# Five token tiles for six meet all experts, and the gathered rows serve three tiles and the samples

## What is computed

```python
s = jnp.einsum('thpd,hpnd->thpn', q, sub_keys)
top_s, top_i = lax.top_k(s, PEER_TOPK)
cand_s = top_s[:, :, 0, :, None] + top_s[:, :, 1, None, :]
cand_i = top_i[:, :, 0, :, None] * PEER_KEYS + top_i[:, :, 1, None, :]
...
fin_s, pos = lax.top_k(cand_s, PEER_TOPK)
fin_i = jnp.take_along_axis(cand_i, pos, axis=-1)
gate = jax.nn.softmax(fin_s, axis=-1)
...
act = jax.nn.gelu(jnp.einsum('tkd,td->tk', expert_u[ik], xk))
return jnp.einsum('tk,tkd->td', gk * act, expert_v[ik])
```

## Time and profile before

| | us |
|---|---|
| median of three runs | 3489.68 |
| the profiled execution | 3483.48 |
| its span | 3481.6 |
| TensorE busy | 3275.2 (94%) |
| TensorE weight loads | 2876.5 (83%) |
| VectorE busy | 2557.4 (73%) |
| ScalarE busy | 922.7 (27%) |
| GpSimd busy | 807.6 (23%) |
| moved | 695.59 MB |

### The profile page before, as it was taken

How to read it: one execution, slowest core, us unless ns; L and a number is a source line. 1 busy time by engine, 2 the same in 40 slices (tenths; PEclk the granted TensorE clock), 3 DMA queues, 4 the chain that set the end, 5 groups by cost and what they waited for, 6 DMA issues and landing times. The chain is left out here.

```text
span 3481.6 us, 46050 instructions
## 1 busy us (share of the span) xinstructions
PE 3275.2 (94%) x17777; PEld 2876.5 (83%) x17777; DVE 2557.4 (73%) x5373; ACT 922.7 (27%) x1336; POOL 807.6 (23%) x639
## 2 busy tenths in 40 slices
PE   6999989689999999989999999976999999999996
PEld 5867755389999999989999999975888888888885
DVE  4621253421299999988888888866899888989986
ACT  3210300311122222224444444432222222222222
POOL 1000000000001110113333333322344443444431
PEclk8999989799999999999999999998999999999998
DMA  5020021211134444448889889878888888888884
GB/s 93 16 38 27 13 96 53 91 56 39 41 128 144 144 143 142 144 137 274 305 286 332 305 299 329 285 279 317 302 303 293 298 304 303 295 299 300 305 298 135
DMA packets 329539, 695.59 MB, mean 200 GB/s; under 512 B 30869, under 2 KB 191449, under 8 KB 323161
## 3 DMA queue, kind: packets, MB, share of 16 engines
q1 hardware_dynamic: 244824, 386.01, 32.2%
q0 software_dynamic: 84496, 306.64, 26.4%
HBM read 580.12 MB, written 110.64 MB: 198 GB/s over the span
## 5 line engine op out<-in xcount | busy, mean ns | idle before, releaser
L1731 POOL DMA_INDIRECT dr_row<-in_peer_v_dram,idx x288 | 425.7, 1478 | 665.9 <-DVE acc_s L1750 655.0
L1731 POOL DMA_INDIRECT gr_row<-in_peer_u_dram,idx x240 | 290.4, 1210 | 464.2 <-DVE raw L1740 442.0
L1750 DVE SCALAR_TENSOR_TENSOR acc_s<-dr_row,gate,acc_s 128x1024 f32<-128x1024 f32 x288 | 367.2, 1275 | 0.0
L2263 DVE TENSOR_TENSOR acc<-pd_po,acc 128x512 f32<-128x512 f32 x384 | 264.0, 687 | 120.7 <-PE pd_po L2296 120.7
L1740 DVE CUSTOM_DVE_ANT_0 gr_row<-gr_row,xs 128x1024 f32<-128x1024 f32 x240 | 288.3, 1216 | 0.0
L2149 ACT ACTIVATE pg_wb<-pg_pw 128x512 f32<-128x512 f32 x192 | 210.8, 1099 | 56.6 <-PE pg_pw L2127 51.2
L486 PE MATMUL fr_a<-pj_w,h_t 128*128 128x256 f32 (+1 forms) x864 | 198.4, 392 | 17.3 <-PEq L184 17.3
L2106 DVE TENSOR_SCALAR pg_hot_i<-pg_iota,sel_t 128x128 f32<-128x128 f32 x768 | 212.8, 355 | 0.0
L486 PEld LDWEIGHTS fr_a<-pj_w,h_t 128*128 128x128 f32 (+1 forms) x864 | 170.3, 227 | 45.0 <-issue 23.1
L2127 PE MATMUL pg_pw<-pg_hot_i,pg_hot_j 128*128 128x128 f32 x1536 | 203.3, 276 | 3.0 <-DVE pg_hot_i L2106 3.0
L2127 PEld LDWEIGHTS pg_pw<-pg_hot_i,pg_hot_j 128*128 128x128 f32 x1536 | 194.8, 192 | 3.4 <-DVE pg_hot_i L2106 3.4
(11 more groups left out here) (487 smaller groups left out, 7972.0 us busy)
## 6 DMA issues: line engine op xcount, KB each, us to landing
pd_v<-in_peer_v_dram SPq DMA_DIRECT2D x128, 512.0 KB
w_d<-pg_wb SPq DMA_DIRECT2D x48, 1024.0 KB
pd_w<-w_d SPq DMA_DIRECT2D x64, 768.0 KB, 6.8
pd_a<-act_d SPq DMA_DIRECT2D x64, 768.0 KB, 9.2
ta_u<-in_peer_u_dram SPq DMA_DIRECT2D x64, 512.0 KB
ga_u<-in_peer_u_dram SPq DMA_DIRECT2D x64, 512.0 KB
act_d<-ta_a SPq DMA_DIRECT2D x128, 192.0 KB
act_d<-ga_a SPq DMA_DIRECT2D x128, 192.0 KB
```

What stands on the lines that cost most here:

```text
L1731: pool.indirect_dma_start(self.buf[i % self.n][:], None, self.table, bass.IndirectOffsetOnAxis(ap=self.idx[:, col:col + 1], axis=0)).then_ ...
L1750: self.nc.vector.scalar_tensor_tensor(out=out, in0=self.buf[i % self.n][:], scalar=w[:, col:col + 1], in1=out, op0=ALU.mult, op1=ALU.add). ...
L2263: nc.vector.tensor_tensor(out, po[(OUTS * g + o) % NPO][:], out, ALU.add).then_inc(o_added, 1)
```

## The change

ND goes from 6 to 5 and NSP from 2 to 3; the widths follow (TD 640, WB 320, COLS 416, BANKS 160, OUTS 10, ten chunks of w_d). The numbers 7 and 14 of the choice become UP_A_TILE = 8 and 16, so that 73 expert tiles run beside the choice and 55 in the gates. The gates loop counts steps of the expert tiles (165) and not groups; groups_at gives a step its groups such that all 160 are made in the first 147 steps; the last chunk is written at step 149. In the down stage SP loads four tiles ahead of acc, GpSimd waits for three products before its first fetch, and the twelve preparations of a group are spread over ten outputs. A buffer that holds the keys and then sel_t gets a shared room. TensorE's and ScalarE's loops in the gates are rewritten like VectorE's.

```diff
-ORDER = (2, 3, 4, 5, 6, 7, 0, 1, 8)
-ND = 6
+ORDER = (3, 4, 5, 6, 7, 0, 1, 2, 8)
+ND = 5
 TD = ND * P
-NSP = 2
+NSP = 3
...
-UP_TOPK = 7 * NT + 1
+UP_A_TILE = 8
+UP_TOPK = UP_A_TILE * NT + 1
 UP_GATES = NK - UP_TOPK
...
-CHOICE = (6, 7, 8, 0, 1, 2, 3, 4, 5)
+CHOICE = tuple(range(ND, NT)) + tuple(range(ND))
+NS = NT - ND
...
-    return min(2 * (UP_TOPK - 2), 14 * q + 14 * (point + 1) // POINTS)
+    return min(2 * (UP_TOPK - 2), 2 * UP_A_TILE * q + 2 * UP_A_TILE * (point + 1) // POINTS)
...
-                if q > 3:
-                    pe.wait_ge(stored, q - 3)
+                if q > NS:
+                    pe.wait_ge(stored, q - NS)
...
+STEPS = 3 * UP_GATES
+EARLY = 18
+
+
+def groups_at(s):
+
+    return range(min(BANKS, BANKS * s // (STEPS - EARLY)), min(BANKS, BANKS * (s + 1) // (STEPS - EARLY)))
...
-            for g in range(BANKS):
-                n, k = g // 3, g % 3
-                if n < UP_GATES:
-                    if k == 1:
-                        up.keep(sp, n, 0)
-                        if n + 2 < UP_GATES:
-                            up.load(sp, n + 2)
-                    if k == 2:
-                        up.keep(sp, n, 1)
-                c, b = g // BC - 1, g % BC
-                if c >= 0 and b < PIECES:
-                    if b == 0:
-                        sp.wait_ge(stored, (c + 1) * BC)
-                    write(c, b)
-            sp.wait_ge(stored, BANKS)
-            for piece in range(PIECES):
-                write(NCH - 1, piece)
+            for s in range(STEPS):
+                n, k = s // 3, s % 3
+                if k == 1:
+                    up.keep(sp, n, 0)
+                    if n + 2 < UP_GATES:
+                        up.load(sp, n + 2)
+                if k == 2:
+                    up.keep(sp, n, 1)
+                for g in groups_at(s):
+                    c, b = g // BC - 1, g % BC
+                    if c >= 0 and b < PIECES:
+                        if b == 0:
+                            sp.wait_ge(stored, (c + 1) * BC)
+                        write(c, b)
+                if s == STEPS - EARLY + 2:
+                    sp.wait_ge(stored, BANKS)
+                    for piece in range(PIECES):
+                        write(NCH - 1, piece)
...
+            for s in range(STEPS + 2):
+                if s < STEPS:
+                    for g in groups_at(s):
+                        one_hots(g)
...
+                    for i in range(NR * s // STEPS, NR * (s + 1) // STEPS):
                         rows_u.dot(dve, i, xs, raw)
...
-            load(0)
-            load(1)
+            for m in range(GE):
+                load(m)
             for s in range(ND):
...
-            for m in range(2, NK):
+            for m in range(GE, NK):
                 load(m)
...
             nc.gpsimd.memset(acc_s[:, NSP, :], 0.0).then_inc(accs_zero, 1)
+            pool.wait_ge(mul, GE - 1)
             for i in range(COLS):
                 rows_v.fetch(pool, i)
...
-                    m = GE * (g + 1) + o // 3
-                    if m < NK:
-                        (multiply, low_v, low_w)[o % 3](m)
+                    for p in range(3 * GE * o // OUTS, 3 * GE * (o + 1) // OUTS):
+                        m = GE * (g + 1) + p // 3
+                        if m < NK:
+                            (multiply, low_v, low_w)[p % 3](m)
                     add(g, o)
```

More of the change, by code:

```diff
@@ L1858, in _ @@
                     exponent(ex_after[n])
-                for q in range(3, NT):
+                for q in range(NS, NT):
                     if turned_after(q) == n:
@@ L1993, in _ @@
                 settle()
-                if q > 3:
-                    dve.wait_ge(turned, q - 3)
+                if q > NS:
+                    dve.wait_ge(turned, q - NS)
                 for i in range(2):
@@ L2095, in _, with one_hots @@
             dve.wait_ge(shaped, 1)
[L2096 to L2110, removed]
+            def one_hots(g):
+                if g >= NHB:
+                    dve.wait_ge(made, g - NHB + 1)
+                hb = g % NHB
+                nc.vector.tensor_tensor(hot_j[:, hb], iota[:].unsqueeze(1).broadcast_to([P, BT, P]),
+                                        sel_t[:, 1, g * BT:(g + 1) * BT].unsqueeze(2).broadcast_to([P, BT, P]),
+                                        ALU.is_equal)
+                for j in range(BT):
+                    tok = slice(g * BT + j, g * BT + j + 1)
+                    ins = nc.vector.tensor_scalar(hot_i[:, hb, j, :], iota[:], sel_t[:, 0, tok], sel_t[:, 2, tok],
+                                                  ALU.is_equal, ALU.mult)
+                ins.then_inc(hot, 1)
+            for s in range(STEPS + 2):
+                if s < STEPS:
+                    for g in groups_at(s):
+                        one_hots(g)
+                n, k = (s - 2) // 3, (s - 2) % 3
+                if s >= 2 and k == 1 and n + 1 < UP_GATES:
                     up.low(dve, n + 1, 0)
                     up.low(dve, n + 1, 1)
-                if g < BANKS:
-                    for i in range(NR * g // BANKS, NR * (g + 1) // BANKS):
+                if s < STEPS:
+                    for i in range(NR * s // STEPS, NR * (s + 1) // STEPS):
                         rows_u.dot(dve, i, xs, raw)
@@ L2121, in _ @@
                 up.turn(pe, 0, half)
[L2122 to L2126, removed]
-                    mm = nc.tensor.matmul(pw[g % 2][:, j, :], hot_j[:, g % NHB, j, :], hot_i[:, g % NHB, j, :],
-                                          start=True, stop=True)
-                mm.then_inc(made, 1)
-                n, k = g // 3, g % 3
-                if n < UP_GATES:
-                    if k == 0:
-                        up.up(pe, n, 0)
-                    if k == 1 and n + 1 < UP_GATES:
-                        up.turn(pe, n + 1, 0)
-                        up.turn(pe, n + 1, 1)
-                    if k == 2:
-                        up.up(pe, n, 1)
+            for s in range(STEPS):
+                for g in groups_at(s):
+                    pe.wait_ge(hot, g + 1)
+                    if g >= 2:
+                        pe.wait_ge(stored, g - 1)
+                    for j in range(BT):
+                        mm = nc.tensor.matmul(pw[g % 2][:, j, :], hot_j[:, g % NHB, j, :], hot_i[:, g % NHB, j, :],
+                                              start=True, stop=True)
+                    mm.then_inc(made, 1)
+                n, k = s // 3, s % 3
+                if k == 0:
+                    up.up(pe, n, 0)
+                if k == 1 and n + 1 < UP_GATES:
+                    up.turn(pe, n + 1, 0)
+                    up.turn(pe, n + 1, 1)
+                if k == 2:
+                    up.up(pe, n, 1)
         @block.scalar
```

45 lines of the change are left out of this document (23 added, 22 removed).

## The result

The changed kernel takes **3566.28 us** (median of 4 runs, 3559.26 to 3571.14), the one before 3491.23 beside it: ratio 1.021, 95% interval 1.0183 to 1.0237. It is 75 us slower; 3473 was predicted, the range ended at 3530, and "slower" had 0.24. The profiled execution took 3571.14 us, its span 3569.3.

What follows compares the result with a forecast made beforehand. The prediction took VectorE to bound the gates and down loops after the change. Its terms, norm and scores +1, choice +8, gates +18, boundary -8, down stage -36, finish 0, sum to -17: 3473 us, range 3425 to 3530.

Steps and rivals of the forecast that it cites:

- 582: Gates loop: TensorE's busy time after the change, forecast at 582 us for 763.
- Norm, choice, boundary, the start of the down stage: Norm and scores +1 us, choice +8, boundary -8; in the down stage TensorE starts near 20 us, VectorE adds from 33.
- Gates loop, +18: Gates loop: 786 us for 768, from VectorE's 754, 12 at the end and 20 for rows late during w_d writes.
- It suffices in the 147 steps and not in the last 18: Gates: five buffers bring a row each 1.52 us, against 2.14 asked in 147 steps and 1.34 in the last 18.
- The turn of 1.52 us: Gates: five buffers turn in 7.6 us (landing 4.8, POOL wait 1.63, dot 1.15), 1.52 us a row.
- rival C: Gates: landings over 7.9 us make VectorE wait at every dot, +100 instead of +18; whole kernel 3555 us; chance 0.12.
- Down stage, -36: Down stage: 1072 us against about 1108, with VectorE as the bound; ends -48 and -10.
- Then 1025 of VectorE, 6 at the end: Down stage: after VectorE's first add at 33 us, 1025 us of its work, 6 at the end, 8 for late rows.
- wrong altogether if TensorE's clock falls in its new gaps: Both loops: a sign that would refute the forecast, given no size and no chance.
- The 8 us for late rows: Down stage: 8 us allowed for late rows, a row each 2.49 us against the turn of 1.52; ends 0 and 30.
- Rival D: Transfer engines bound both loops, full at 344 GB/s: gates 820 us, down 1091, sum +36, 3526 us; chance 0.20.

Runs made afterwards that it cites:

- the run with the pieces apart: The changed kernel with the four pieces of each w_d chunk written 4 groups apart, not at consecutive groups: 3541.97 us, ratio 1.0158.
- the dummies: The changed kernel with 20 matmuls of constants into a spare PSUM bank after each group's outputs in the down stage: 3518.47 us, ratio 1.0069.
- the mends: Seven gates row buffers, preparations by eighth output, w_d pieces 4 groups apart, one-hots 6 steps ahead: 3444.76 us; old division, five buffers, other three: 3445.27 us.
- the mended change: The changed kernel with seven gates row buffers, preparations by the eighth output, w_d pieces 4 groups apart, one-hots 6 steps ahead: 3444.76 us, ratio 0.9858.
- old division in the new structure: The changed kernel with six dense tiles, two gathered, seven expert tiles beside each choice as before, the rest of the change kept: 3486.14 us, ratio 0.9991.

## Why the prediction was wrong

**What bounds the kernel after.** Right: VectorE, in both loops. TensorE ceased to be the bound, though its busy time was underrated: 637 us in the run without row transfers (583.67 + 53.60), where 582 stood; that run's granted clock there was 0.95 to 0.97, and the sum had supposed full clock.

**Norm, choice, boundary, the start of the down stage.** Right within 3 us each: +3, +7, -11. TensorE started 20 us after the down stage's start, as forecast. VectorE's first add came 39 us after it where 33 stood: the sum counted the bytes up to accumulators and rows, but ahead of the first add stands the fifth tile's product, whose loads come behind them (VectorE waited 17.8 us for its activations, until 2448.61).

**Gates loop, +18.** The step that failed is the pace of the rows: "It suffices in the 147 steps and not in the last 18", with 2 us lost for each chunk and 12 at the end; 60 and 29 us were paid where 20 and 12 were allowed. The turn of 1.52 us took its landing from the quiet choice (4.8 us) into a stage at share 0.92. The change's trace gives no landing for these rows; that of the run with the pieces apart does:

```profile
DMA to landing us min/median/max: 4.8/7.2/16.0
```

Five rows are asked for in 5 x 2.14 = 10.7 us in the steps with one-hots, in 6.7 in the last 18. A landing of 7.2 and a dot of 1.15 fit into the first and not into the second, and the longest landing fits into neither. Since one late row holds VectorE and the four fetches behind it, the typical landing was the wrong number; the long ones count. The prediction had the place right, behind the writes of the chunks, and the size too small: 51.6 us in nine clusters of waits, 5.7 a chunk.

The 1.63 us that the turn and rival C's 7.9 us also count is a misreading of the earlier trace rows. It is GpSimd's idle time before that fetch, while it waited for the dot; the fetch starts 0.35 us behind the dot's end, in the trace of the kernel before (its end here, the fetch's start at 1807.09 in the earlier trace rows):

```profile
1806.74 0.08 DVE L1740 DVE_READ_ACCUMULATOR2_ANT raw<- 128x1 f32 x1
```

Without it the turn would have come out shorter still, so this is not what failed. Rival C named the mechanism and its 3555 came nearest, in part by luck: it supposed a steady wait at every dot and +100 in the gates, where 61 of 368 dots waited and +69 were paid, and it had no loss in the down stage.

**Down stage, -36.** The step that failed is the sum behind the first add at 33 us: "Then 1025 of VectorE, 6 at the end" and 8 for late rows. It has no term for TensorE. Its busy time of 890 was compared with VectorE's 1036 as a total, and a sum hides an order: in the ten outputs of a group TensorE must wait for VectorE's last preparation and VectorE for TensorE's next output. The lower clock then made that output 4.9 us long for 2.72. The prediction had written "wrong altogether if TensorE's clock falls in its new gaps" and gave it no price and no chance. Its price is 48 us (the dummies), half the miss. Without it the stage took 1077 to 1079 against 1072, of which the later first add is 4 to 6. The 8 us for late rows were not needed: VectorE waited for none in this stage of the change.

**Rival D.** Refuted: 370 GB/s over 754 us at share 0.98, above the 344 at which it saw the engines full. It also stands above the 358 GB/s of the Trainium skill, "DMA: Bandwidth & Descriptors", section "Where 436 GB/s comes from"; the measurement decides.

**The division's worth.** What was never asked: whether the same time was to be had without moving a tile. With the mends the two divisions are within 1 us of each other, 3444.76 and 3445.27 (ratios 0.9858 and 0.9877, with intervals that overlap). TensorE's relief changed the engine that bounds and not the bound: the gates loop takes 754 us in the new division, with VectorE busy 747 of them, and 757 in the old one, with TensorE busy 756 of 758.

What stays open: how the waits for rows that spacing the pieces left (35 us of 54 up to the last one-hots, with five buffers) divide between the load of the writes and that of everything else, and where the gates of the old division gained with one-hots 6 instead of 18 ahead.

## What to carry to other kernels

When work moves off the engine that bounds, look at what that engine's new idle time is made of: here pieces of 4.5 us before each group cost TensorE its clock, and the output behind them was on the path of the engine that bounds now. Put what it waits for some outputs earlier, or keep it busy with matmuls into a spare bank.

A ring of buffers is sized by the longest landing under the new load and the fastest stretch of demand, not by the mean of either; test it with two buffers more before anything else. And try each mend on the kernel before as well: here the 45 us that the mended change gains over the kernel before were to be had, within the noise, without moving a tile.

## What the runs showed of the hardware

- After each of 29 stops of 4.53 us TensorE's matmuls of 512 columns started 0.43 us apart for some 4.4 us, then 0.23. With preparations by the eighth output there were 30 stops of 2.3 to 5.6 us: after 28 the spacing went to 0.43, at once or up to five matmuls later, and after two of 3.5 us it stayed at 0.23. After the 29 of 0.5 to 1.9 us behind 20 dummies it was never above 0.31. The Trainium skill, "TensorE: Matmul & The Clock Gate", section "Why this matters for your kernels", advises against idle gaps between bursts of matmuls; the traces agree but for those two stops.
- Its two levels gave the down stage a mean granted clock of 0.90 in the change, 0.93 with preparations by the eighth output, and 0.99 with dummies; the last two took the same time, 1079 and 1077 us. The mean clock tells nothing until it is known which outputs are waited for.
- The core moved 370 GB/s for 754 us, and 403 over 19 us (old division in the new structure, 2371 to 2390), where the two loops of the kernel before ran at 299 and 296 and had not asked for more; the earlier trace rows has 406 over 25 us.
